# Two output projections computed from fp32r halves, modulation sums spread between low parts, three modulation chunks moved

## The reference

```python
mod = (silu(c) @ w_ada[i] + b_ada[i]).reshape(b, 6, d)     # i = 0, 1: layers three and four
x = x + g_m * (mixer(hm) @ w_out)                          # g_m is one of the six rows
```

## Time and profile before

| | us |
|---|---|
| three runs | 1511.5, 1513.54, 1516.96; median 1513.54 |
| the profiled execution, its own time | 1510.9 |
| its span | 1509.2 |
| PE busy | 1410.7 (93%) |
| VectorE busy | 736.5 (49%) |
| ScalarE busy | 496.6 (33%) |
| granted TensorE clock, mean over the span | 0.984 of full |

### The profile page before, as it was taken

How to read it: one execution, slowest core, us unless ns; L and a number is a source line. 1 busy time by engine, 2 the same in 40 slices (tenths; PEclk the granted TensorE clock), 3 DMA queues, 4 the chain that set the end, 5 groups by cost and what they waited for, 6 DMA issues and landing times. The chain is left out here.

```text
span 1509.2 us, 23584 instructions
## 1 busy us (share of the span) xinstructions
PE 1410.7 (93%) x9090; PEld 766.4 (51%) x9090; DVE 736.5 (49%) x1659; ACT 496.6 (33%) x996; POOL 103.0 (7%) x258
## 2 busy tenths in 40 slices
PE   8999999997899899999888997899799998989998
PEld 4486533332365645333226885788554337755432
DVE  1468332222255545222226765675576346669534
ACT  3222221111216403111116656665613126661211
POOL 0000021110000001111102000200001102000110
PEclk9999999999999999999999999999999999999999
DMA  8996989999974269999998463335369998437996
GB/s 365 366 348 265 405 360 411 420 420 421 427 301 167 97 290 370 398 422 420 421 423 347 168 251 112 112 140 192 116 243 419 420 425 324 162 119 296 422 420 247
DMA packets 63400, 469.80 MB, mean 311 GB/s; under 512 B 7809, under 2 KB 15921, under 8 KB 18738
## 3 DMA queue, kind: packets, MB, share of 16 engines
q1 hardware_dynamic: 63282, 468.22, 76.7%
HBM read 465.42 MB, written 2.76 MB: 310 GB/s over the span
## 5 line engine op out<-in xcount | busy, mean ns | idle before, releaser
L1663 PE MATMUL PS<-ring,catT 128*32 128x512 f32 x3072 | 347.9, 594 | 11.8 <-issue 10.9
L826 PE MATMUL PS<-w_split,h_split 128*128 128x512 f32 x1152 | 270.9, 394 | 6.0 <-DVE w_split L911 5.9
L826 PEld LDWEIGHTS PS<-w_split,h_split 128*128 128x128 f32 x1152 | 214.1, 188 | 56.5 <-DVE w_split L911 8.6
L1663 PEld LDWEIGHTS PS<-ring,catT 128*32 128x32 f32 x3072 | 96.0, 110 | 227.5 <-issue 227.2
L911 DVE TENSOR_TENSOR w_split<-ring,w_split 128x512 fp32r<-128x512 f32 x192 | 132.7, 706 | 67.3 <-ACT w_split L859 67.1
L1686 PE MATMUL PS<-ring,row_place 128*32 128x512 f32 x1232 | 141.8, 593 | 14.1 <-issue 14.1
L859 ACT CAST w_split<-ring 128x512 fp32r<-128x512 f32 x192 | 118.3, 621 | 104.5 <-PE PS L826 104.1
L1873 ACT ACTIVATE row_place<-PS 128x256 f32<-128x256 f32 x48 | 18.5, 385 | 359.7 <-PE PS L1663 359.7
L508 PE MATMUL PS<-ring,catT 128*128 128x512 f32 x224 | 96.7, 592 | 1.0 <-PEq L1022 1.0
L1686 PEld LDWEIGHTS PS<-ring,row_place 128*32 128x32 f32 x1232 | 40.9, 110 | 105.0 <-issue 104.4
L1556 POOL COPY catT<-xsT 128x256 f32 x176 | 63.3, 403 | 393.0 <-PE PS L1663 385.4
(11 more groups left out here) (445 smaller groups left out, 1829.4 us busy)
## 6 DMA issues: line engine op xcount, KB each, us to landing
ring<-in_moe SPq DMA_DIRECT2D x269, 1024.0 KB, 14.3
ring<-in_w_ada SPq DMA_DIRECT2D x16, 3072.0 KB, 13.0
ring<-in_a_w_in SPq DMA_DIRECT2D x23, 2048.0 KB, 10.4
ring<-in_b_w_in SPq DMA_DIRECT2D x8, 2048.0 KB, 22.5
first_down<-in_moe SPq DMA_DIRECT2D x8, 1024.0 KB, 8.4
ring<-in_a_w_out SPq DMA_DIRECT2D x2, 3072.0 KB, 15.2
ring<-in_b_w_out SPq DMA_DIRECT2D x2, 3072.0 KB, 16.5
ring<-in_w_mem_kv SPq DMA_DIRECT2D x2, 2048.0 KB, 11.6
```

The source lines that it names most:

```text
L826: last = nc.tensor.matmul(PS[:, 2 * (i % 2) + t, :], hs[:, hp, k, t * P:(t + 1) * P], wk[:, (KT * i + k) % splits, wp, :], start=k == 0 an ...
L1663: last = nc.tensor.matmul(PS[lanes, 4 + i % 2, :].rearrange("p (g f) -> p g f", g=2), xf[:, i % 2, k, lanes], gate_up_weights(2 * i + q % ...
```

## The change

The edits. (1) The second and third layers' output projections use a new function, `project_rows_split`, on three fp32r products. (2) Two ada chunks (8, 9) are summed in it one `tensor_tensor_reduce` at a time, after each second low part; in the third layer's it sums none. (3) ada 9 now stands ahead of the second layer's second chunk instead of behind it; ada 10 and 11 move from the third layer's output projection into its input projection (ahead of each half's last chunk), ada 12 into the fourth layer's. (4) `project_heads_split` sums these, each after a named low part, and loads `silu_row`.

```diff
-        c_bout = weight_amid("b_w_out", 12, [512] * 2, [1, 0], 1)
+        c_bout = weight_amid("b_w_out", 12, [512] * 2, [1, 1])
-        c_ain2 = weight("a_w_in_2", 8, [512] * 18)
-        c_aout2 = weight_amid("a_w_out_2", 8, [512] * 2, [1, 0], 2)
+        c_ain2 = weight_amid("a_w_in_2", 8, [512] * 18, [0] * 8 + [1] + [0] * 8 + [1])
+        c_aout2 = weight("a_w_out_2", 8, [512] * 2)
-        c_bin2 = weight("b_w_in_2", 8, [512] * 3 + [16] + [512] * 3)
+        c_bin2 = weight_amid("b_w_in_2", 8, [512] * 3 + [16] + [512] * 3, [0] * 6 + [1])
...
+        def project_rows_split(srcT, k, first, gate, router, after, gain=None, shift=None, splits=4, sums=()):
+                squares = PS[:, 6, :] if sums else silu_row[:, 0:BANK]
+                by_pool = [n for n in range(k, 2 * k) if sums and n % 3 == 2]
+                HELD = 3
...
+                @block.gpsimd
+                    for j in range(k):
+                        pool.wait_ge(*(h_odd if j % 2 and not sums else h_even).at(j + 1 if sums else j // 2 + 1))
+                        nc.gpsimd.tensor_tensor(hs[:, 1, j, :], srcT[:, j, :], hs[:, 0, j, :].bitcast(F32), ALU.subtract).then_inc(h_low.sem, 1)
+                    for n in by_pool:
+                        pool.wait_ge(*w_high.at(n + 1))
+                        low_part(nc.gpsimd, n).then_inc(w_low_pool.sem, 1)
...
+                @block.tensor       # k-tile by k-tile, both token tiles; the last three k-tiles token tile by token tile
+                        for j in range(held):
+                            if c == 0:
+                                pe.wait_ge(*(h_odd if j % 2 and not sums else h_even).at(j + 1 if sums else j // 2 + 1))
+                            pe.wait_ge(*w_high.at(k * c + j + 1))
+                            for t in range(TT):
+                                product(c, j, t, 0, 0)
+                            pe.wait_ge(*low_made(k * c + j))
+                            for t in range(TT):
+                                product(c, j, t, 0, 1)
+                            if c == 0:
+                                pe.wait_ge(*h_low.at(j + 1))
+                            for t in range(TT):
+                                last = product(c, j, t, 1, 0)
+                            last.then_inc(w_used.sem, 1)
...
+                @block.scalar
+                    nc.scalar.activation(stat[:, 2, 30:31], ones_f[:, 0:1], ACT.Sqrt)
+                    for j in range(0, k, 2):
+                        nc.scalar.copy(hs[:, 0, j, :], srcT[:, j, :]).then_inc(h_even.sem, 1)
+                        high(0, j)
+                        if sums:
+                            nc.scalar.copy(hs[:, 0, j + 1, :], srcT[:, j + 1, :]).then_inc(h_even.sem, 1)
+                        high(0, j + 1)
...
+                @block.vector
+                    def low(c, j):
+                        if n in by_dve:
+                            dve.wait_ge(*w_high.at(n + 1))
+                            low_part(nc.vector, n).then_inc(w_low.sem, 1)
+                        if sums and j % 2 == 1:
+                            last = ada_sum(sums[c], j // 2, silu_row)
...
+                    if sums:
+                        dve.wait_ge(*silu_loaded.at(16))
+                    for j in range(0, k, 2):
+                        if not sums:
+                            nc.vector.tensor_copy(hs[:, 0, j + 1, :], srcT[:, j + 1, :]).then_inc(h_odd.sem, 1)
+                        low(0, j)
+                        low(0, j + 1)
+                        if j == 4:       # gate row copied out of PSUM, then the modulation
+                            after()
+                    for j in range(k):
+                        low(1, j)
+                        if j == splits - 1:
+                            add(0)
+                        if j == splits:
+                            add(1)
...
         def project_heads_split(...):       # behind a low part that sums_behind names
+                            if (i, k) in sums_behind:
+                                last = ada_sum(ada_chunk, m, silu_row)
...
-            project_rows(catT, 12, c_bout, [512] * 2, add_rows(None), ada=[1, 0], ada_last=1, after=lambda: modulation(0, (0, 48), (0, 1)), router=1)
+            project_rows_split(catT, 12, c_bout, None, 1, lambda: modulation(0, (0, 48), (0, 1)), sums=(8, 9))
-                        project_heads_split(hT, c_ain2 + half * 9, jobs, rows=z_rows, load_last=load_two_biases,
+                        project_heads_split(hT, c_ain2 + half * 10, jobs, rows=z_rows, load_last=load_two_biases, ada_chunk=10 + half, sums_behind=((7, 3), (7, 5), (7, 7), (8, 1), (8, 3), (8, 5)),
-            project_rows(catT, 8, c_aout2, [512] * 2, add_rows(grow[:]), ada=[1, 0], ada_last=2, ...
+            project_rows_split(catT, 8, c_aout2, mod[:, 0, 16:24], 2, lambda: modulation(1, (0, 24), (0,)), grow[:], mod[:, 0, 24:32])
+                                    ... side=forget, ada_chunk=12, sums_behind=((1, 5), (2, 5), (4, 4), (5, 1), (5, 3), (5, 5)))
```

More of the change, by code:

```diff
@@ L441, in ada_part, with ada_sum @@
                 nc.vector.sem_inc(chunk_used, 1)
+        def ada_sum(c, m, row):
+            w = stream.view(ada_at[c], 6)
+            return nc.vector.tensor_tensor_reduce(w[:, m, :], w[:, m, :], row, 1.0, 0.0, ALU.mult, ALU.add, ada_out[:, 6 * c + m:6 * c + m + 1])
         def modulation(l, n, halves):
@@ L741, in project_heads, with project_heads_split @@
                 s.passed(k)
-        def project_heads_split(srcT, first, jobs, splits=3, rows=None, norm=None, side=None, load_last=None):
+        def project_heads_split(srcT, first, jobs, splits=3, rows=None, norm=None, side=None, load_last=None, ada_chunk=None, sums_behind=()):
             turns = [i for i, job in enumerate(jobs) if job["hd"]]
@@ L756, in project_heads_split @@
                 wk = sbuf(st, "w_split", [P, splits, 2, 512], F32R)
-                h_even, h_odd, h_low = sig("ph_source_high"), sig("ph_source_high_odd"), sig("ph_source_low")
+                h_even, h_odd, h_low = sig("ph_source_high"), sig("ph_other_part"), sig("ph_source_low")
                 w_high, w_low, w_used = sig("ph_weight_high"), sig("ph_weight_low"), sig("ph_weight_used")
@@ L767, in turned_x @@
                     return PS[:, 4 + 2 * (k % 2) + k // 4, at:at + T]
+                silu_row = catT[:, 8:12, :].rearrange("p k n -> p (k n)") if side is None else sbuf(st, "silu_row", [P, D])[:]
                 def chunk(i):
-                    return first + i + (1 if side is not None and i >= 3 else 0)
+                    return first + i + (1 if side is not None and i >= 3 else 0) + (1 if i >= len(jobs) - 1 else 0)
                 def col16(q):
@@ L778, in _ @@
                     if side is not None:
+                        load_silu_row(silu_row)
                         stream.issue(nc, sp, chunk(3))
@@ L889, in _ @@
                             nc.scalar.activation(stat[:, 2, col16(q)], stat[:, 1, col16(q)], ACT.Sqrt).then_inc(root_ready.sem, 1)
+                            if side is None and i == turns[-1]:
+                                nc.scalar.dma_start(silu_row, A["silu_dram"].to_broadcast([P, D])).then_inc(silu_loaded.sem, 16)
                         if i - 1 in turns:
@@ L958, in project_heads_split @@
                 s.passed(k)
+            silu_loaded.passed(16)
             for s in (w_high, w_low, w_used):
@@ L3106, in build @@
                         dilated_attention([head(h) for h in range(8)], bias, bias_load)
-            project_rows(catT, 8, c_aout2, [512] * 2, add_rows(grow[:]), ada=[1, 0], ada_last=2, after=lambda: modulation(1, (0, 24), (0,)), router=2, gate=mod[:, 0, 16:24], shift=mod[:, 0, 24:32])
+            project_rows_split(catT, 8, c_aout2, mod[:, 0, 16:24], 2, lambda: modulation(1, (0, 24), (0,)), grow[:], mod[:, 0, 24:32])
         if stop >= 7:
```

110 lines of the change are left out of this document (109 added, 1 removed).

## The result

The changed kernel takes 1526.0 us (median of 10 runs, 1519.0 to 1530.2), the kernel before on the same chip 1511.8 (10 runs): ratio 1.0101, interval 1.0082 to 1.0121. It is slower by 14 us where I forecast 1.7 faster, and it lies above the whole range. A second set of six runs of the changed kernel gave 1522.1 and a ratio of 1.0085 (1.0065 to 1.0105).

What follows compares the result with a forecast made beforehand. PE, busy for 93% of the span, was taken to set the end nearly everywhere. 1.8 + 4.7 - 1.3 - 3.5 = 1.7 us gained from 1513.5 gave 1511.8, stated as 1511.9; range 1504.5 to 1519.

Steps and rivals of the forecast that it cites:

- Step 6: Third layer, second half's attention: chunks queued ahead make bias tiles late, 3.5 us lost, between 1.6 and 5.3.
- step 2: Start of the second layer's output projection: 4.6 us lost by a later start, 2.0 by the clock's fall.
- Step 3: VectorE inside the second layer's output projection: two low parts and a sum fit by 0.2 us, costed at nothing.
- rival C: VectorE becomes the bound in the second layer's output projection: 4.3 us worse than forecast, 1516.2 us; chance 0.27.
- Step 5: Sums in the input projections: nothing in the third layer (0.5 us a half at most), 1.3 us lost in the fourth.
- step 1: Products of the output projections, split instead of plain: 8.4 us saved in the second layer, 5.6 in the third.
- step 4: Third layer's output projection: 5.6 us saved less 0.9 lost, a gain of 4.7, with 3.7 and 5.0 as ends.
- Step 7: Experts: the second layer's gain of 1.8 us passes through; more pieces in the ring gain the third layer's nothing.
- Rival B: Third layer's attention: the bias tiles are in time, 3.5 us more gain, 1508.4 us; chance 0.30.

Runs made afterwards that it cites:

- a3_only_ada12: The kernel before with only modulation chunk 12 moved into the fourth layer's input projection, its six sums at the changed kernel's places: 1517.1 us, ratio 1.0044.
- b3_pool_short: a1_tiles_first with GpSimd making only 16 of 256 columns of each source low part in the second layer's output projection: 1509.1 us, ratio 0.9986.
- a1_tiles_first: The changed kernel with the third layer's second-half expert pieces issued at the output projection, behind the bias tiles: 1511.4 us, ratio 1.0006 to the kernel before.

## Why the prediction was wrong

**Step 6, the moved chunks on SP's queue, failed in size**, and it decides the sign: I took 3.5 us, between 1.6 and 5.3, and the stage lost 9.2 and 10.0 in the two profiles, and some 12 to 14 by the ratios. The chain was right link by link: the twelve places, the rate of 0.42 MB per us, the backlog's end (1074 forecast, 1077.5 measured in a kernel that came 3.2 us later), VectorE at the wait, PE waiting for all of it. Two terms were not. I gave the tiles 1.9 to 5.7 us from the end of the backlog; they landed 7.1 us behind it. Their own bytes are 4.2 us of this, inside my bounds; the rest is that I took the end of the backlog for one moment, while some engines were on ring chunks for 2 to 3 us more. And I did not carry the wait on to the clock, though the earlier trace rows showed what a pause costs and step 2 had it priced: 2.5 us here, the twice longer products at 1087. Of the distance between the stage and the ratios, 1 to 5 us in the five runs with late tiles, the lower mean clock is all that I can show; in which stages it falls from run to run stays open.

**Step 3, VectorE inside the second layer's projection, failed.** I costed it at nothing with a cover of 0.2 us; it costs some 4 us, and that is rival C, which had 4.3. With it the split form is 1.6 us slower there than the plain one; C's sum had 2.5. The row that says so stood in the earlier trace rows: 1.81 us for two low parts beside GpSimd. Its premise, that the sums take turns with GpSimd too, is what b3_pool_short's rows show, in both directions. In the first column half it is mostly not the sum that gets longer: it makes GpSimd wait, and GpSimd's subtraction then stands in the time of the next two low parts: so 1.8 us for 1.3 in four pairs of six, and 2.4 in one. The Trainium skill's rule (SBUF — State Buffer, "Who interferes with whom"), that the two exclude each other for a whole instruction, agrees with these rows (1.15 us for 0.22, 2.32 for 1.21), and I had given it a chance of 0.27 for want of a row with a sum in it.

**Step 5, the sums in the input projections**: right in the third layer (106.6 us in the second half before and after), and 2.9 for 1.3 in the fourth, inside the bounds. The three sums among the row norms were priced at 0.2, 0.6 and 0.5 us; in a3_only_ada12 PE's three new waits are 0.93, 0.66 and 0.71, and 0.6 are spread over the rest. Of the 0.93 VectorE's wait for chunk 12 is 0.84, a term that my sum did not have: I had asked what the moved chunks do to other transfers, and not whether chunk 12 itself would be there for its first sum.

**Steps 1, 2 and 4 were right.** The third layer's projection gained 4.4 us (forecast 4.7), of which some 1.6 went again behind the stage at a lower clock, which no step had. At the start of the second layer's stage PE's stream begins 5.6 us behind attention's last product in b3_pool_short for 1.05 before, so 4.5 (forecast 4.6), and the clock took 1.9 more (142 products in 34.42 us for 32.5; forecast 2.0). With hardly any work of GpSimd's beside it the projection gains 2.6 us for my 1.8. **Step 7** can't be judged: equal kernels differ by 6.6 us over that stretch. Rival B, the tiles in time, is what a1_tiles_first made of it, and the result, 1511.4, shows that even then C and the fourth layer would have eaten the gain.

Of the cases, C was the true one, and its time of 1516.2 was short by what steps 5 and 6 lacked: 1516.2 + 5.7 + 1.6 is 1523.5, between the two medians measured. That it comes so close is in part luck: C's own term was 0.9 too dear, and the 1.6 us given back in the third layer are in no term. The range ended at 1519 because the tiles' upper end, 5.3 us, was taken from a row in which nothing stood ahead of them.

## What to carry to other kernels

When a chunk is moved, count the bytes that now stand ahead of every small transfer issued later, from the layout, and add to the backlog's end its uneven tail over the engines, the tiles' own time at the rate of small packets, and the clock behind the wait; ask the same of the moved chunk, whether it will be there for its own first use; a look-ahead that nobody needs yet is best stopped in front of transfers that somebody will. Before giving an engine a third instruction per step, price each at its length beside its busiest neighbour: a cover of 7% is no cover when a row shows one of them at 1.4 times its length. Extra instructions belong where the timeline shows the engine idle ahead of a wait that comes anyway; six of them cost 2.9 us at one set of places, 0.8 of it for a chunk that had not landed, and 0.6 at another.

## What the hardware showed that I had not expected

Transfers issued from a second engine's queue did not get ahead of a backlog on the first: they landed 7.5 us after it thinned out, with 0.12 MB of the 2.21 that moved from 1072 to 1078. The issuing engine itself stood for 5.84 us in four issues, where a single one had taken 0.6; SP stood for 11.13 us in six, for 3.98. The bias tiles, in packets of 1 KB, move at 180 to 190 GB/s when nothing else is under way, where the ring's chunks in packets of 8 KB move at 420. And a GpSimd instruction on 16 columns can take 1.15 us for 0.22, when VectorE is in a long one with two inputs.
